# A two-layer backbone on one core: scan products behind the attention steps, rows turned tile by tile

## What is computed

```python
h  = rmsnorm(x) * (1 + scale1) + shift1
P  = h @ w_in                       # columns for four mixers
# A: differential attention, 4 heads, weights p1 - lam * p2
# B: gated linear recurrence in both directions, 4 heads, state 64 x 64
# C: neighbourhood attention on the latent grid, 4 heads
# D: real part of a 2-D DFT
x  = x + gate1 * concat(A, B, C, D) @ w_out
h2 = rmsnorm(x) * (1 + scale2) + shift2
x  = x + gate2 * moe(h2)            # 16 experts, two for each token
```

## Time and profile before

| what | us |
|---|---|
| median of 3 runs | 1281.07 (1279.88 to 1282.71) |
| the profiled execution | 1280.95 |
| its span from first to last instruction | 1279.1 |
| attention and scan loop, layer 0 | 125 to 285 |
| experts, layer 0 | 362 to 636 |
| between the layers | 636 to 662 |
| attention and scan loop, layer 1 | 746 to 906 |
| experts, layer 1 | 984 to 1253 |

### The profile page before, as it was taken

One profiled execution on the slowest core, in us unless ns is written; L12 is line 12 of the kernel. 1 busy time (PEld: TensorE's weight loads), 2 busy tenths in 40 slices (PEclk: granted clock), 3 DMA queues, 4 the chain that ended last, 5 costly groups with the idle time before them and its releaser, 6 DMA issues.

```text
span 1279.1 us, 19883 instructions
## 1 busy us (share of the span) xinstructions
PE 1187.2 (93%) x7830; PEld 542.6 (42%) x7830; DVE 522.3 (41%) x1267; ACT 429.5 (34%) x740; POOL 229.7 (18%) x339
## 2 busy tenths in 40 slices
PE   4999899899899999999989989988998999999994
PEld 1555555454433333333354655555444333333331
DVE  1384667733522122111365747575244122122217
ACT  2223444431332333333421434352222432333333
POOL 1230274210011110010200325441200011110000
PEclk9999889889899999999999998997998999999997
DMA  9839531565799999999740312055715999999971
GB/s 364 298 145 167 108 99 66 214 230 226 299 345 407 386 388 386 395 388 381 285 177 1 140 66 92 8 215 217 304 56 207 361 397 385 399 393 388 393 299 80
DMA packets 52242, 324.79 MB, mean 254 GB/s; under 512 B 7825, under 2 KB 8241, under 8 KB 33600
## 3 DMA queue, kind: packets, MB, share of 16 engines
q1 hardware_dynamic: 39296, 293.16, 59.2%
q0 software_dynamic: 11584, 25.79, 8.1%
q10 hardware_dynamic: 1280, 4.72, 0.9%
HBM read 318.50 MB, written 24.09 MB: 268 GB/s over the span
## 4 chain that ended last, share of the span: by engine, by line
PE 71%; DVE 14%; DMA 10%; issue 2%; ACT 1%; SPq 0%; DVEq 0%; ACTq 0%; POOLq 0%
PE ps L1944 33%; PE ps L1577 12%; DMA ring<-moe_w_up 7%; PE ps L1633 7%; PE ps L1834 7%; PE ps L1593 3%; DVE attT L1174 3%; PE ps L1933 3%; PE ps L1616 2%; DMA ring<-ada_w 2%; DVE dbuf L1151 2%; PE ps L1728 1%; DVE small L1279 1%; PE ps L1757 1%; DVE dbuf L1146 1%
## 5 line engine op out<-in xcount | busy, mean ns | idle before, releaser
L1944 PE MATMUL ps<-ring,dbuf 128*32 128x512 f32 x3072 | 426.0, 593 | 4.2 <-DMA ring<-moe_w_up 1.9
L1944 PE MATMUL ps<-extra,dbuf 128*32 128x512 f32 x1536 | 206.6, 592 | 1.9 <-DMA ring<-moe_w_up 1.9
L1944 PEld LDWEIGHTS ps<-ring,dbuf 128*32 128x32 f32 x3072 | 118.4, 110 | 199.9 <-issue 194.2
L1577 PE MATMUL ps<-ring,extra 128*128 128x512 f32 (+1 forms) x384 | 149.0, 548 | 0.0
L1944 PEld LDWEIGHTS ps<-extra,dbuf 128*32 128x32 f32 x1536 | 60.2, 110 | 131.8 <-issue 131.6
L1000 ACT ACTIVATE big<-ps 96x512 f32<-96x512 f32 x32 | 34.5, 1077 | 224.1 <-issue 167.5
L1633 PE MATMUL ps<-extra,ring 128*128 128x384 f32 x320 | 108.9, 499 | 0.0
L759 POOL DMA_INDIRECT expert_rows<-big,lst x28 | 26.3, 941 | 427.2 <-DVE big L1457 411.8
L1577 PEld LDWEIGHTS ps<-ring,extra 128*128 128x128 f32 x384 | 73.7, 193 | 69.3 <-issue 65.8
L1435 DVE COPY dbuf<-ps 128x384 f32<-128x384 f32 x32 | 17.8, 558 | 200.2 <-PE ps L1933 200.2
L1834 PE MATMUL ps<-ring,extra 128*128 128x512 f32 x192 | 84.3, 594 | 3.0 <-DVE extra L1344 1.8
(11 more groups left out here) (280 smaller groups left out, 1460.6 us busy)
## 6 DMA issues: line engine op xcount, KB each, us to landing
ring<-moe_w_up SPq DMA_DIRECT2D x30, 2048.0 KB
ring<-ada_w SPq DMA_DIRECT2D x24, 2048.0 KB
ring<-moe_w_down SPq DMA_DIRECT2D x18, 2048.0 KB
ring<-moe_w_gate SPq DMA_DIRECT2D x16, 2048.0 KB
extra<-moe_w_gate SPq DMA_DIRECT2D x16, 2048.0 KB
extra<-moe_w_down SPq DMA_DIRECT2D x14, 2048.0 KB, 18.0
ring<-w_in SPq DMA_DIRECT2D x12, 2048.0 KB
ring<-w_out SPq DMA_DIRECT2D x4, 2048.0 KB
```

Of the source, the lines that this page charges most:

```text
L1577: ins = pe.matmul(out, a, b, start=(n == 0), stop=(n == len(pairs) - 1))
L1944: return pe.matmul(p[QT * g:QT * (g + 1), :], a, w, start=start, stop=stop, tile_position=(0, QT * g))
```

## The change

- In the loop, on TensorE, VectorE and ScalarE alike, each step now does the attention step first, then the dense blocks, and then what belongs to the scan unit (key turn, grams, key-value product; placing, states, operands; key copies, decays). Four dense blocks move from g = 2 to g = 3. `layer_jobs` follows the new order, and so do the banks.
- At the start, six of the eight chunks are turned after the second ada block, the other two in the midst of the first z product. The filler calls there go from 3, 1, 2, 0 to 3, 0, 1, 0.
- Between the layers, results are returned tile by tile; rows of a tile are turned as soon as the tile is normalised, in two halves of four chunks, with filler calls of 3 and 4 between in place of 9. ScalarE scales both halves of tile 0 and the second halves of tiles 1 and 2, VectorE the first halves of tiles 1 and 2. The scales of the next layer are formed at the start of the experts.

```diff
+EARLY_CHUNKS = 6
+TILE_BANKS, AFTER_TILES = [5, 0, 1, 3, 6, 2], 4
...
-DENSE = {(0, 0): [("cq", 0)], (0, 2): [("cq", 1)], (1, 0): [("ck", 0)], (1, 2): [("ck", 1)], (2, 0): [("cvdu", 0)],
-         (2, 2): [("cvdu", 1)], (3, 0): [("cvdu", 2)], (2, 1): [("cc",)], (3, 1): [("bo", 0)], (3, 2): [("du",)], (3, 3): [("dy",), ("nk",)],
-         (4, 0): [("ada", 0)], (4, 1): [("ada", 1)], (4, 2): [("ada", 2)], (5, 0): [("ada", 3)], (5, 1): [("ada", 4)],
+DENSE = {(0, 0): [("cq", 0)], (0, 3): [("cq", 1)], (1, 0): [("ck", 0)], (1, 3): [("ck", 1)], (2, 0): [("cvdu", 0)],
+         (2, 3): [("cvdu", 1)], (3, 0): [("cvdu", 2)], (2, 1): [("cc",)], (3, 1): [("bo", 0)], (3, 2): [("du",)], (3, 3): [("dy",), ("nk",)],
+         (4, 0): [("ada", 0)], (4, 1): [("ada", 1)], (4, 3): [("ada", 2)], (5, 0): [("ada", 3)], (5, 1): [("ada", 4)],
...
 def layer_jobs(l):
...
-    jobs = [("mod", 0)] if l == 0 else []
-    jobs += [("hT", 2 * l, k) for k in range(KC)]
-    jobs += [("z", l, d, hp) for d in range(2) for hp in range(HP)] + [("aqk", l, t) for t in range(NT)]
+    z = [("z", l, d, hp) for d in range(2) for hp in range(HP)]
+    if l == 0:
+        chunks = [("hT", 0, k) for k in range(KC)]
+        jobs = chunks[0:EARLY_CHUNKS] + [("mod", 0), z[0]] + chunks[EARLY_CHUNKS:] + z[1:]
+    else:
+        jobs = z
+    jobs += [("aqk", l, t) for t in range(NT)]
...
     for u in range(NUNIT):
-        jobs += [("kd", l, u)]
...
-            jobs += [("gram", l, u, h2, g // 2) for h2 in range(2)] if g in (0, 2) else []
-            jobs += [("kv", l, u)] if g == 1 else []
...
+            jobs += [("kd", l, u)] if g == 0 else []
+            jobs += [("gram", l, u, h2, g // 2) for h2 in range(2)] if g in (0, 2) else []
+            jobs += [("kv", l, u)] if g == 1 else []
...
     for l in range(L):
+        if l:
+            for i, b in enumerate(TILE_BANKS):
+                uses[b] += 1
+                place[("hT", 2 * l, i // 2, i % 2)] = (b, uses[b])
+            n = AFTER_TILES
...
+            def modulate_half(l, t, b):
+                act.wait_ge(s_mod, 2 * l + 1)
+                job, s = ("hT", 2 * l, t, b), min(t, 1)
+                p = ready(act, job)
+                for n in range(4):
+                    k = 4 * b + n
+                    ins = act.activation(hT[:, k, t * P:(t + 1) * P], p[:, n * P:(n + 1) * P], ACT.Identity, scale=A1[:, 0, k, s:s + 1],
+                                         bias=modv[:, l, k, s:s + 1])
+                    if n < 3:
+                        step(ins)
+                release(act, ins, job)
             def modulate(l):
...
             for l in range(L):
-                sum_squares(2 * l)
...
+                    sum_squares(0)
...
-                modulate(l)
+                    modulate(0)
+                else:
+                    squares_of(2 * l, 0)
+                    squares_of(2 * l, 1)
+                    modulate_half(l, 0, 0)
+                    modulate_half(l, 0, 1)
+                    squares_of(2 * l, 2)
+                    modulate_half(l, 1, 1)
+                    modulate_half(l, 2, 1)
...
                 for u in range(NUNIT):
-                    keys_out(u)
...
-                        if g == 1 and 2 <= u + 1 < NUNIT:
-                            decays(u + 1)
...
+                        if g == 0:
+                            keys_out(u)
+                        if g == 1 and 2 <= u + 1 < NUNIT:
+                            decays(u + 1)
...
+            def modulate_half(l, t, b):
+                job, s = ("hT", 2 * l, t, b), min(t, 1)
+                p = ready(dve, job)
+                for n in range(4):
+                    k = 4 * b + n
+                    ins = dve.tensor_scalar(hT[:, k, t * P:(t + 1) * P], p[:, n * P:(n + 1) * P], A1[:, 0, k, s:s + 1],
+                                            modv[:, l, k, s:s + 1], ALU.mult, ALU.add)
+                    if n < 3:
+                        step(ins)
+                release(dve, ins, job)
             def modulate(l):
...
-                scales(l, 0)
-                modulate(l)
+                    scales(0, 0)
+                    modulate(0)
+                else:
+                    modulate_half(l, 1, 0)
+                    modulate_half(l, 2, 0)
...
                 for u in range(NUNIT):
...
+                        attend(PER_UNIT * u + g)
+                        for what in DENSE.get((u, g), []):
+                            if what[0] == "mod":
+                                modulation(group(*BETWEEN[l][what[1] - 1]))
...
+                        if g == 2 and u + 1 < NUNIT:
+                            operands(l, u + 1, range(4))
...
-                        attend(PER_UNIT * u + g)
-                        if g == 2 and u + 1 < NUNIT:
-                            operands(l, u + 1, range(4))
-                        for what in DENSE.get((u, g), []):
-                            if what[0] == "mod":
-                                modulation(group(*BETWEEN[l][what[1] - 1]))
...
+                    scales(l + 1, 0)
...
-            def hidden(n):
-                pe.wait_ge(s_xn, NT * (n + 1))
-                for k in range(KC):
-                    transposes(("hT", n, k), [xn[:, t, k * P:(k + 1) * P] for t in range(NT)])
+            def hidden(chunks):
+                pe.wait_ge(s_xn, NT)
+                for k in chunks:
+                    transposes(("hT", 0, k), [xn[:, t, k * P:(k + 1) * P] for t in range(NT)])
+            def turned_tile(l, t):
+                pe.wait_ge(s_xn, NT * 2 * l + t + 1)
+                for b in range(2):
+                    transposes(("hT", 2 * l, t, b), [xn[:, t, k * P:(k + 1) * P] for k in range(4 * b, 4 * b + 4)])
...
             def by_token(l, w, job, t, c0, c1):
...
             def by_feature(l, w, job, c):
...
-                    if job[0] == "z":
-                        moved(pe, ("hT", 2 * l, k))
+                    if job == ("z", 0, 0, 0):
+                        if k == EARLY_CHUNKS:
+                            hidden(range(EARLY_CHUNKS, KC))
+                        moved(pe, ("hT", 0, k))
+                    if job == ("z", 1, 0, 0) and k % 4 == 0:
+                        for t in range(NT):
+                            moved(pe, ("hT", 2, t, k // 4))
...
             for l in range(L):
...
-                    for j, n in zip(ADA_FIRST, (3, 1, 2, 0)):
+                    for j, n in zip(ADA_FIRST, (3, 0, 1, 0)):
...
+                        if j == 1:
+                            hidden(range(EARLY_CHUNKS))
...
-                hidden(2 * l)
...
                 for u in range(NUNIT):
-                    decayed_keys(u)
...
+                        attend(PER_UNIT * u + g)
+                        for what in DENSE.get((u, g), []):
+                            dense(what)
+                        if g == 0:
+                            decayed_keys(u)
...
-                        attend(PER_UNIT * u + g)
-                        for what in DENSE.get((u, g), []):
-                            dense(what)
...
-                for t in range(2):
+                for t in range(NT):
...
-                for kind in ("dn0", "dn1"):
-                    moved(pe, (kind, l), NE - 1)
-                returned(0, 1)
-                returned(1, 1)
-                for b in range(2):
-                    begin(pe, ("cm", l, 2, b))
-                returned(2, 0)
-                returned(2, 1)
+                    if t == 0:
+                        for kind in ("dn0", "dn1"):
+                            moved(pe, (kind, l), NE - 1)
+                    returned(t, 1)
...
-                    keep_running(9)
+                    keep_running(3)
+                    turned_tile(l + 1, 0)
+                    keep_running(4)
+                    turned_tile(l + 1, 1)
+                    turned_tile(l + 1, 2)
```

## The result

The changed kernel takes **1311.6 us** (median, 1309.3 to 1314.3) against 1281.4 (1279.9 to 1282.7): ratio 1.0236, interval 1.0215 to 1.0258. It is slower, as forecast, but by 30 us, not by 7, and lies above the range. The profiled execution is the slowest of the four (1314.3 us), so its pieces add up to a little more than the medians differ by: its span is 1312.4 us, 33.3 more than before.

A forecast was written before the change was run, and what follows sets the result against it. TensorE's waits and slow clock were taken to bound it. Loops +6.4, start +2.5, between layers +0.5 and end -1.9 made +7.5: 1288.5 us. Forecast slower, 1284 to 1300 (chance 0.58); without the outermost fifth, 1273 to 1300.

The forecast's parts named there:

- What bounds the kernel: Whole kernel: 71% of the span lies on TensorE, so a change pays only where TensorE waits or runs slowly.
- Waits of the loop: Both loops: waits on operands go, new ones come; 20.1 us of waits against 15.5, so +4.6 a loop.
- unit 2: Third scan unit, second step: TensorE waits 2.1 us while VectorE places scores and does an attention step first.
- steps 12 to 18: Late loop: VectorE waits in step 16 for GpSimd's squares, so TensorE waits 8.6 us, mostly in one piece over 6.
- unit 4: Loop, fifth scan unit: outputs of steps 16 and 17 wait some 2.2 us for copies behind two table loads.
- Clock of the loop: Both loops: four waits each bring a slow stretch like the 3.4 us one; 13.6 against 15.0, so -1.4 a loop.
- The bound of +7 a loop: Upper bound for one loop: one more slow stretch at the loop head and one in unit 4.
- Start: From 0 to 46 us: earlier turns, but TensorE waits and slows; +2.5 us, bounds +0.3 and +3.3.
- Between the layers and end: Between layers +0.5 us, bounds -2 and +1.5; end -1.9, as VectorE's first addition no longer waits 1.76.
- Table loads: ScalarE: 1.28 us a load as in the trace, against the skill's 2.66 us a switch, which would give 1294.
- the clock holds: Rival, chance 0.14: waits of 1.9 to 3.0 us in units 0 to 2 leave 2.4 GHz standing; 1271 us.
- The squares come in time: Rival, chance 0.12: GpSimd is done when VectorE reaches step 16; about -8 us a loop, 1272 us.

The follow-up runs named there:

- experiment 4: Changed kernel with GpSimd's sum of bias and mask cut in eight instructions: 1307.2 us, ratio 1.0202.
- experiment 5: Old loop order, with start, boundary and end as changed, plus unread filler products in TensorE's loop waits: 1264.8 us, ratio 0.9877.
- experiment 6: Experiment 4 plus fillers at the loop head and in steps 2, 6 and 10, in the bank of the modulation rows: 1294.5 us, ratio 1.0108.
- experiments 1 to 7 and 11: Follow-up kernels with the changed start; those not named singly: only the loop order undone (1285.0 us), and fillers in the new order's waits (1309.0 us).
- Experiment 9: Experiment 5 plus three fillers ahead of z in the bank of the modulation rows: 1263.1 us, ratio 0.9856.
- experiment 7: Experiment 4 with the squares of mixer A put ahead of the exponents of unit 5 in GpSimd's list: 1302.1 us, ratio 1.0155.
- experiment 2: Changed kernel with the four dense blocks back at g = 2: 1347.2 us, ratio 1.0514.
- experiment 11: New loop order with experiment 4, experiment 6 and experiment 7 joined, and fillers in steps 16 and 18 too: 1289.1 us, ratio 1.006.
- experiment 8: Changed kernel with three fillers ahead of z, in z's own bank: 1315.3 us, ratio 1.026.
- experiment 10: Experiment 5 with the old start and fillers of 1, 1 and 2 more between the layers: 1258.9 us, ratio 0.9823.

## Why the prediction was right in its sign and wrong in its size

- **What bounds the kernel**: right. Time went only where TensorE waits or runs slowly.
- **Waits of the loop**: right in sum, in part by luck. Forecast +4.6 a loop, measured +5.8. One by one, forecast and measured in the first loop: loop head 1.9 and 1.78, unit 0 3.0 and 2.85, unit 1 2.7 and 1.96 (0.17, 1.52, 0.27), unit 2 2.1 and 5.70 (0.39, 5.31), unit 3 1.1 and 1.20, steps 12 to 18 8.6 and 5.61 (2.66, 2.95), unit 4 2.2 and 1.50. Two were off and cancelled. In unit 2 I had left out that GpSimd's sum moves along with the exponents it follows, and what it does to VectorE: 4.1 us, shown by experiment 4. In steps 12 to 18 I had all of the GpSimd chain on TensorE; L1355 did wait 4.49 us for the squares, but TensorE had turns and a block of its own left:

```profile
256.74 0.95 DVE L1355 TENSOR_REDUCE small<-extra 128x12 f32<-128x768 f32 x1 [4.49 <-POOL extra L713]
```

- **Clock of the loop**: the step that failed. I wrote that "the waits of 3.0, 2.7, 2.1 and over 6 us each bring a slow stretch like the 3.4 us one: 13.6 against 15.0: -1.4". It was +10.8 and +8.7. Half of TensorE's busy time at half clock, an estimate of its cost, makes 26.8 us for the seven stretches of the first loop, where I had 13.6 for four (before it makes 15.0; the busy times themselves grew by 10.8). One half of the miss is the price: the four that I had foreseen cost 3.5, 5.2, 5.8 and 5.7 us (20.2), not 3.4 each. I had taken the price from one place, where the dense block followed 4.3 us behind the wait, and kept it while the change moved small products between them; the trace of before had a stretch of 10 us as well. The other half is the number: three more stretches, at the loop head, in unit 3 and behind the 2.66 us at 248.37, cost 6.6 us together. That this half clock lay on the way is shown by the fillers: they took 10 us off a loop in experiment 5 and 7.5 and 6.0 in experiment 6, three quarters and somewhat over half of what they took off TensorE's products.
- **The bound of +7 a loop** went with it: it allowed two more stretches of 3.4 us, not three, and no longer ones.
- **Start**: sign right, +4.6 instead of +2.5, above the bound. In the profiles of experiments 1 to 7 and 11, whose start is the same, the last keys are turned at 127.3 to 129.1 us, 2.9 to 4.7 later than before. "z begins at 39.8 instead of at 40.6" was wrong: TensorE waited for the block of w_in until 40.6, and half clock came behind these 2.79 us (6.73 for 3.98, so 2.75 lost), not behind the third ada block. Experiment 9 takes back 1.3. The six turns and the wait for chunk 6 (0.82 and 0.83) were 1.65 where I had 1.41; and my own terms, 0.66 and 0.75 less 0.8, make +0.6 and not +0.5.
- **Between the layers and end**: right, +0.2 and -1.7 for +0.5 and -1.9; at the end the 1.76 us went, but the second wait of 0.17, which I had counted as gone, is still there. The 1.0 us less from the loop to the returned rows in layer 0 says nothing: the same piece takes 354.9 to 358.7 us in the profiles of the experiments.
- **Table loads**: the trace of after has 1.28 us a load again, and the decays begin 1.29 us after the start of theirs. The 2.66 us of the Trainium skill (ScalarE: Activation LUTs, What ACT_TABLE_LOAD costs) are not seen.
- **Rivals**: "the clock holds" is what experiment 6 makes by hand; of itself it did the opposite. "The squares come in time" (8 us a loop): experiment 7 gave some 4 in the piece that it touches and 5.1 in the whole time, and the rest went into the copies behind the table loads, which I had priced for unit 4 alone.

What stays open: what brings the clock back. A near dense block goes with a short stretch, but the rise at 845 came without one, as did the one at 661 between the layers before, behind turns alone, and experiment 2, which moved the dense blocks alone, brought waits with it. Nor does a run tell what of the 7 to 8 us of waits and fillers in experiment 11 better placed fillers would save. The filler of experiment 8 was not the test of the start that it was meant to be; experiment 9 was, in another kernel.

## What to carry to other kernels

Price a wait by what follows it: with the clock in play, a wait costs its length and up to half of the time at half clock behind it (half to three quarters of that was won back here), and stretches at half clock were longer where small products lay between the wait and the next dense block. Count every wait as one that may lower the clock, the short ones too. Before reordering, fill: dense products that nobody reads, written to a bank that is free at that moment, took 1.6% off here (1285.0 to 1264.8) where the new loop order cost 2.1% (1285.0 to 1311.6); a filler whose bank is still held stands behind the wait and adds its length. Where a list in order is moved, follow every instruction behind it, a large GpSimd one above all, to what it now lies beside.

## What the hardware did that was not expected

- TensorE without a gap for 9.04 us (scores, turns, outputs, grams) stayed at 1.2 GHz, as for 6.00 us in another place; in both the clock rose while the next dense block ran. At the same place in the second loop it rose at 845 after 5.2 us of the same small products, with no dense block.
- The length of a wait did not tell alone whether the clock falls: 1.76 us did it at the start of before, while 1.99 and 2.00 us at the same stage did not in experiment 10 and in the changed kernel, and at 234 in the loop it fell behind waits of 0.45 and 0.75 with small products between.
- One VectorE operation on two elements took 4.25 us beside one GpSimd instruction of 4.49, and 0.56 once that was cut in eight.
